# Accumulating scatters of a mixture-of-experts stage: one chain over two tables, or one chain for each table

## The reference, cut to what matters

```
h   = RMSNorm(x) * (1 + scale_f) + shift_f            # 1032 x 1024
experts, weights = top 6 of 64 by a sigmoid router    # 6 of 64 for each token
for each block of rows that go to one expert e:
    y = (silu(rows @ w1[e]) * (rows @ w3[e])) @ w2[e] # 1024 -> 256 -> 1024
    routed[token of the row] += y * weight
x   = x + gate_f * (shared_expert(h) + routed)
out = RMSNorm(x) * g_final
```

## Time and profile before

| | |
|---|---|
| median of 3 runs | 1570.03 us (1564.13 to 1572.75) |
| the profiled execution | 1567.41 us |
| its span, from the first to the last instruction | 1565.6 us |
| granted TensorE clock, mean over the span | 0.967 of full speed |
| PE busy | 1441.4 us, 92% |
| DVE busy | 832.3 us, 53% |
| POOL busy | 492.7 us, 31% |
| moved by DMA | 369.69 MB, mean 236 GB/s |

### The profile page before, as it was taken

The page is one execution under the profiler, slowest core; times in us unless marked ns, Lnnn a source line. Parts: engine busy times, 40 slices in busy tenths (PEclk is TensorE's granted clock), DMA queues, the critical chain, the costliest instruction groups (busy, mean ns, idle before and its releaser), DMA issues.

```text
span 1565.6 us, 17523 instructions
## 1 busy us (share of the span) xinstructions
PE 1441.4 (92%) x5855; PEld 642.1 (41%) x5855; DVE 832.3 (53%) x2113; ACT 217.7 (14%) x369; POOL 492.7 (31%) x426
## 2 busy tenths in 40 slices
PE   5899999999999999989899999999989999999947
PEld 2344454554445454644333344433323333333313
DVE  1047778999979899856233333333323243333227
ACT  1111321313121321322000000000000000000003
POOL 0001010111212111215345454545544544554410
PEclk9999999999999999988899999999999999999978
DMA  9987202202121001511999999999999999999976
GB/s 333 325 315 289 84 27 97 79 32 84 41 71 41 19 29 42 170 56 49 341 307 370 364 374 366 375 363 355 367 369 351 375 362 375 331 341 329 375 228 247
DMA packets 93436, 369.69 MB, mean 236 GB/s; under 512 B 17741, under 2 KB 29425, under 8 KB 68207
## 3 DMA queue, kind: packets, MB, share of 16 engines
q1 hardware_dynamic: 69383, 304.29, 50.0%
q0 software_dynamic: 23968, 64.35, 16.5%
HBM read 323.10 MB, written 62.13 MB: 246 GB/s over the span
## 4 chain that ended last, share of the span: by engine, by line
DMA 39%; PE 28%; DVE 19%; issue 8%; SPq 4%; ACT 2%; POOL 0%; POOLq 0%; DVEq 0%; ACTq 0%
DMA acc_rows<-W,kT 18%; DMA acc_rows<-xr,kT 13%; PE U L652 9%; DVE cv L1260 7%; PE R L705 7%; PE U L862 4%; DMA acc_rows<-xr,shared_f 4%; SPq L401 2%; PE R L878 2%; DMA W<-in_w_ada 1%; DMA x_t<-h_rows,q_r 1%; PE R L616 1%; SPq L408 1%; PE U L811 1%; DVE R L1272 1%
## 5 line engine op out<-in xcount | busy, mean ns | idle before, releaser
L652 PE MATMUL U<-W,hT 128*128 128x512 f32 x864 | 385.4, 600 | 1.2 <-issue 1.2
L1260 DVE SCALAR_TENSOR_TENSOR cv<-win,cw,cv 128x128 f32<-128x128 f32 x960 | 254.9, 345 | 1.4
L878 PE MATMUL R<-W,glu 128*32 128x512 f32 (+2 forms) x1024 | 240.9, 597 | 1.3 <-DVE glu L1552 1.3
L862 PE MATMUL U<-W,hT 128*128 128x512 f32 (+2 forms) x784 | 236.4, 606 | 5.1 <-issue 5.1
L652 PEld LDWEIGHTS U<-W,hT 128*128 128x128 f32 x864 | 162.5, 193 | 188.3 <-issue 188.3
L862 PE MATMUL U<-W,cat 128*32 128x512 f32 (+2 forms) x1264 | 236.2, 603 | 0.0
L1539 DVE STREAM_TRANSPOSE hT<-x_t 128x1024 f32<-128x1024 f32 x33 | 67.2, 2036 | 207.4 <-DMA x_t<-h_rows,q_r 174.1
L1539 DVE STREAM_TRANSPOSE cat<-W 128x1024 f32<-128x1024 f32 x33 | 67.7, 2051 | 198.9 <-DMA W<-h_rows,q_r 198.9
L878 PEld LDWEIGHTS R<-W,glu 128*32 128x32 f32 (+2 forms) x1024 | 83.9, 138 | 151.4 <-issue 149.9
L1734 POOL DMA_INDIRECT W<-h_rows,q_r x128 | 129.1, 1009 | 53.5 <-issue 53.5
L862 PEld LDWEIGHTS U<-W,hT 128*128 128x128 f32 (+2 forms) x784 | 90.8, 158 | 126.7 <-issue 125.4
(11 more groups left out here) (293 smaller groups left out, 1173.6 us busy)
## 6 DMA issues: line engine op xcount, KB each, us to landing
W<-in_w SPq DMA_DIRECT2D x192, 1024.0 KB, 17.2
W<-in_w_ada SPq DMA_DIRECT2D x24, 1024.0 KB, 8.8
W<-in_w_in SPq DMA_DIRECT2D x6, 2048.0 KB, 20.0
W<-acc_rows SPq DMA_DIRECT2D x16, 512.0 KB, 9.7
h_rows<-xr SPq DMA_DIRECT2D x9, 512.0 KB, 2.7
x_t<-in_x_prompt SPq DMA_DIRECT2D x8, 512.0 KB
W<-in_w_out SPq DMA_DIRECT2D x1, 4096.0 KB, 17.2
xr<-in_x_prompt SPq DMA_DIRECT2D x8, 512.0 KB
```

Source lines behind the costliest of these rows:

```text
L652: last = mm(U[BANK[g]][:, :], hT[:, k, :], w_in[:, k, 512 * g:512 * g + 512], start=k == 0, stop=k == KT - 1)
L862: last = mm(U[1][cols, :], xgT[z][:, k, cols], w13[:, :, k, :], start=k == 0, stop=k == KT - 1)
L878: last = mm(R[cols, 512 * half:512 * half + 512], hidT[:, f, cols], weights[:, at:at + 512], start=f == 0, stop=f == FT - 1)
L1260: ins = v.scalar_tensor_tensor(cv[:, c, :], win[:, c, w:w + P], cw[:, c, w:w + 1], cv[:, c, :], ALU.mult, ALU.add)
```

## The change

The two tables become two tensors, `acc_rows[0]` and `acc_rows[1]`, and a plan `PARTS` says for each block which of its quarters go to which table. A block of one expert (and one of the shared expert) goes as one piece to the table that the plan counts free first. A mixed block is cut by its owners into two pieces, the larger first, one to each table, and is scattered by two transfers: each gets all 128 rows and a list of row numbers of its own in which the other piece's rows are far out of bounds. Rows out of bounds are skipped (`oob_is_err=False`), and since the bound is now the number of tokens, filling rows are skipped too. A piece waits only for the pieces before it in the same table (`DONE` counts them), and DVE's evacuation of block x waits until all pieces of block x-2 have landed. In the last stage tiles 0 and 1 get a semaphore each; DVE adds the two halves of tile 0 itself, and PE starts with tile 1. The row numbers of both tables are made by one DVE operation of twice the columns, from a constant of twice the size. SP's waits for the end of the scatters, and the further rounds, count the pieces in the same way.

```diff
+def pieces(x):
+    u = EXEC[x][0]
+    owners = [None] * 4 if u is None else [s for s, _ in QUARTERS[4 * u:4 * u + 4]]
+    first = owners.count(owners[0])
+    return [(0, first)] + [(first, 4 - first)] * (first < 4)
+
+def chains():
+    parts, done, busy = [], [], [0, 0]
+    for x in range(NX):
+        cut = sorted(pieces(x), key=lambda piece: -piece[1])
+        nearer = 0 if busy[0] <= busy[1] else 1
+        taken = [((nearer + i) % 2, at, n) for i, (at, n) in enumerate(cut)]
+        for table, _, n in taken:
+            busy[table] = max(busy[table], 11 * x) + 3 + 2 * n
+        parts.append(taken)
+        done.append(tuple(sum(table == c for block in parts for table, _, _ in block) for c in range(2)))
+    return parts, done
+
+PARTS, DONE = chains()
...
-        acc_in = win_in[0:TP // 2]
-        rows_summed = win_in[TP // 2]
+        acc_in = [win_in[0], win_in[1]] + [win_in[2 + i // 2] for i in range(TP - 2)]
+        acc_there = [16 + 32, 16 + 32] + [16 + 64] * (TP - 2)
+        rows_summed = win_in[5]
...
-        acc_rows = scratch("acc_rows", (2 * TABLE, D))
+        acc_rows = [scratch(f"acc_rows{i}", (TABLE, D)) for i in range(2)]
...
-        slot_i = kT[:, 0, 0:64].bitcast(I32)
+        slot_i = kT[:, 0, 0:2 * NU].bitcast(I32).rearrange("p (c u) -> p c u", c=2)
...
-        slot_base = k_d[:, 192:192 + NU]
+        slot_base = k_d[:, 192:192 + 2 * NU].rearrange("p (c u) -> p c u", c=2)
...
             for i in range(TP):
-                sp.dma_start(acc_t[i], acc_rows[P * i:P * i + P, :]).then_inc(acc_in[i // 2], 16)
-                sp.dma_start(odd_t[i], acc_rows[TABLE + P * i:TABLE + P * i + P, :]).then_inc(acc_in[i // 2], 16)
+                sp.dma_start(acc_t[i], acc_rows[0][P * i:P * i + P, :]).then_inc(acc_in[i], 16)
+                sp.dma_start(odd_t[i], acc_rows[1][P * i:P * i + P, :]).then_inc(acc_in[i], 16)
...
-            for i in range(TP):
-                pe.wait_ge(acc_in[i // 2], 16 + 64)
+            for i in range(1, TP):
+                pe.wait_ge(acc_in[i], acc_there[i])
...
             def blk_y(x):
                 dve.wait_ge(y_done, x + 1)
-                dve.wait_ge(scattered[x % 2], 16 * (x // 2))
+                for c in range(2):
+                    if x > 1 and DONE[x - 2][c]:
+                        dve.wait_ge(scattered[c], 16 * DONE[x - 2][c])
...
-            v.tensor_tensor(slot_i[:, 0:NU], X[:, 0:NU], slot_base, ALU.add).then_inc(slot_ready, 1)
+            v.tensor_tensor(slot_i, X[:, 0:NU].unsqueeze(1).to_broadcast([P, 2, NU]), slot_base, ALU.add).then_inc(slot_ready, 1)
...
             for i in range(TP):
-                dve.wait_ge(sum_done, i + 1)
-                ins = v.tensor_tensor(acc_t[i], (X, R)[i % 2][:, :], gt_f, ALU.mult)
+                if i == 0:
+                    dve.wait_ge(acc_in[i], acc_there[i])
+                    link(v.tensor_tensor(acc_t[i], acc_t[i], odd_t[i], ALU.add))
+                    ins = v.tensor_tensor(acc_t[i], acc_t[i], gt_f, ALU.mult)
+                else:
+                    dve.wait_ge(sum_done, i)
+                    ins = v.tensor_tensor(acc_t[i], (X, R)[i % 2][:, :], gt_f, ALU.mult)
...
             def scatter(x):
                 u, n = EXEC[x]
-                at = shared_i[:, 4 * NT + n:4 * NT + n + 1] if u is None else slot_i[:, u:u + 1]
                 pool.wait_ge(y_evac, x + 1)
-                if x > 0:
-                    pool.wait_ge(scattered[1 - x % 2], 16 * ((x + 1) // 2))
-                pool.indirect_dma_start(acc_rows, bass.IndirectOffsetOnAxis(ap=at, axis=0), y_sbs[x % 2], None,
-                                        bounds_check=2 * TABLE - 1, oob_is_err=True,
-                                        compute_op=ALU.add).then_inc(scattered[x % 2], 16)
+                before = [0, 0] if x == 0 else list(DONE[x - 1])
+                for c, first, n in PARTS[x]:
+                    if before[c]:
+                        pool.wait_ge(scattered[c], 16 * before[c])
+                    before[c] += 1
+                    at = shared_i[:, 4 * NT + EXEC[x][1]:4 * NT + EXEC[x][1] + 1] if EXEC[x][0] is None else slot_i[:, c, EXEC[x][0]:EXEC[x][0] + 1]
+                    pool.indirect_dma_start(acc_rows[c], bass.IndirectOffsetOnAxis(ap=at, axis=0), y_sbs[x % 2], None,
+                                            bounds_check=TOKENS - 1, oob_is_err=False,
+                                            compute_op=ALU.add).then_inc(scattered[c], 16)
...
-        "slot_base": np.array([[TABLE * (QUARTERS[4 * u + p // 32][0] % 2) for u in range(NU)] for p in range(P)]),
+        "slot_base": skips(),
...
+def skips():
+    far = np.full((P, 2, NU), 8.0 * TABLE)
+    for x, (u, _) in enumerate(EXEC):
+        if u is not None:
+            for c, at, n in PARTS[x]:
+                far[32 * at:32 * at + 32 * n, c, u] = 0.0
+    return far.reshape(P, 2 * NU)
```

More of the change, by code:

```diff
@@ L172, in build @@
         ring_in = [sem(f"ring_in{r}") for r in range(RING + 1)]
-        acc_in = win_in[0:TP // 2]
-        rows_summed = win_in[TP // 2]
+        acc_in = [win_in[0], win_in[1]] + [win_in[2 + i // 2] for i in range(TP - 2)]
+        acc_there = [16 + 32, 16 + 32] + [16 + 64] * (TP - 2)
+        rows_summed = win_in[5]
+        assert TP == 8
         sum_done, gated = sem("sum_done"), sem("gated")
@@ L462, in _ @@
                 for x in range(2):
-                    sp.dma_start(acc_rows[bass.ds(i * 2 * P + TABLE * x - 4 * P, 2 * P), :], t["zeros"]).then_inc(spare_in, 16)
+                    sp.dma_start(acc_rows[x][bass.ds(i * 2 * P - 4 * P, 2 * P), :], t["zeros"]).then_inc(spare_in, 16)
                 load_next(i)
@@ L521, in _ @@
             sp.dma_start(disp, t["disp"]).then_inc(disp_in, 16)
-            sp.dma_start(slot_base, t["slot_base"]).then_inc(disp_in, 16)
+            sp.dma_start(k_d[:, 192:192 + 2 * NU], t["slot_base"]).then_inc(disp_in, 16)
             sp.wait_ge(x2_ready, NT)
@@ L556, in _ @@
                         b = rd * NE + s
-                        sp.wait_ge(scattered[1], 8 * NX)
-                        sp.wait_ge(scattered[0], 8 * NX + 16 * b)
+                        sp.wait_ge(scattered[1], 16 * DONE[-1][1])
+                        sp.wait_ge(scattered[0], 16 * DONE[-1][0] + 16 * b)
                         sp.sem_inc(sp_free, 1)
@@ L578, in _ @@
                 sp.dma_start(g_s[rows], t["g_final"].rearrange("(c n) -> c n", n=SW)).then_inc(sample_in, 16)
-            sp.wait_ge(scattered[0], 8 * NX + 16 * NE * rounds)
+            sp.wait_ge(scattered[0], 16 * DONE[-1][0] + 16 * NE * rounds)
             sp.sem_inc(sp_free, 1)
-            sp.wait_ge(scattered[1], 8 * NX)
-            sp.dma_start(acc_s, in_pieces(acc_rows[SEQ:TOKENS, :])).then_inc(sample_in, 16)
-            sp.dma_start(odd_s, in_pieces(acc_rows[TABLE + SEQ:TABLE + TOKENS, :])).then_inc(sample_in, 16)
+            sp.wait_ge(scattered[1], 16 * DONE[-1][1])
+            sp.dma_start(acc_s, in_pieces(acc_rows[0][SEQ:TOKENS, :])).then_inc(sample_in, 16)
+            sp.dma_start(odd_s, in_pieces(acc_rows[1][SEQ:TOKENS, :])).then_inc(sample_in, 16)
             for i in range(TP):
-                sp.dma_start(acc_t[i], acc_rows[P * i:P * i + P, :]).then_inc(acc_in[i // 2], 16)
-                sp.dma_start(odd_t[i], acc_rows[TABLE + P * i:TABLE + P * i + P, :]).then_inc(acc_in[i // 2], 16)
+                sp.dma_start(acc_t[i], acc_rows[0][P * i:P * i + P, :]).then_inc(acc_in[i], 16)
+                sp.dma_start(odd_t[i], acc_rows[1][P * i:P * i + P, :]).then_inc(acc_in[i], 16)
             for i in range(TP):
@@ L1786, in _ @@
                         pool.sem_inc(pool_free, 1)
-                        pool.indirect_dma_start(acc_rows, bass.IndirectOffsetOnAxis(ap=slot_cur, axis=0), y_sbs[0], None,
-                                                bounds_check=2 * TABLE - 1, oob_is_err=True,
+                        pool.indirect_dma_start(acc_rows[0], bass.IndirectOffsetOnAxis(ap=slot_cur, axis=0), y_sbs[0], None,
+                                                bounds_check=TOKENS - 1, oob_is_err=False,
                                                 compute_op=ALU.add).then_inc(scattered[0], 16)
```

## The result

The changed kernel takes 1573.83 us (median of 19 runs, 1570.24 to 1579.82) beside 1568.83 us of the kernel before on the same chips (19 runs, 1564.13 to 1574.75). The ratio is 1.0034, with a 95% interval from 1.0022 to 1.0047: no faster, a little slower. Predicted were 1550.

What follows compares the result with a forecast made beforehand. PE was taken as the bound, with 20.2 us of waits for DVE caused by chained scatters delaying gathers on POOL. −16.0 − 0.5 − 3.4 = −19.9 from 1567.4 gave 1547.5; the median lies 2.6 higher, so 1550, range 1540 to 1567.

Steps and rivals of the forecast that it cites:

- the landing of the second piece: Mixed blocks' second scatter: lands 8.5 us after its start, so the next block's gathers still move up by 2.1 us.
- the other case that I had named: Whole blocks behind mixed ones: if the second piece took 10.4 us by itself, gathers would move up by 0.2 us only.
- the 4.3 us behind mixed blocks: Expert stage: half of the 8.6 us of PE's waits shared to the 28 mixed blocks was to go.
- the forecast with nothing taken off: Case that skipped rows still cost their time: same as the forecast, since the 1224 filling rows were counted at 0.
- 11.6 counted for all 38 one-piece blocks: Expert stage: 38/66 of PE's 20.2 us of waits for DVE, 11.6 us, was to go whole.
- DMA is full: Rival, expert stage: freeing the order moves nothing, only bytes count; −12 − 3.9 us, about 1554; chance 0.17.
- The second piece makes it slower: Rival, mixed blocks: POOL still waits and each second piece delays gathers by 1.91 us; +38, about 1608; chance 0.11.
- Filling rows: Scatters: 1224 rows, 5.0 MB, no longer written; counted at 0, with 12.4 to 19.9 us if DMA is the bound.
- The last stage: After the expert stage: DVE adds tile 0 and takes tile 1 sooner; −3.4 us, bounds −2.5 and −4.5.
- The end of the stage: Last scatters of blocks 64 and 65, both mixed: between +1.3 and −2.7 us, taken as −0.5.
- The signs named: Right: 94 scatters, DVE at tile 1 about 14 us after SP's first load, PE's DVE waits under 5 us.
- The rule against the split: First rival, two-piece scatters: transfers to disjoint partition halves serialize, so the split earns no rate; only order and bytes count.

Runs made afterwards that it cites:

- own rows: Changed kernel with each piece scattered from its own partitions only, no row skipped for the other piece's sake; 1550.83 us, 0.989 of the kernel before.
- the last stage alone: The kernel before with only the last-stage edit (DVE adds tile 0, PE starts with tile 1), scatters as before; ratio 0.9983 to the kernel before.
- second only: Changed kernel with own rows in the second pieces alone, first pieces keeping their skipped rows; ratio 1.0063 to the kernel before.

## Why the prediction was wrong

**The step that failed** is the landing of the second piece: "The two pieces together carry one block's rows, so I let the second land when the whole block would have", 8.5 us after its start. They carry one block's data, but two blocks' rows, and a skipped row is still a packet. It measured 11.1 to 11.7 us, worse than the other case that I had named ("Were the piece to take 10.4 us by itself") and set aside. So nothing came of the 4.3 us behind mixed blocks, nor of the 2.1 us that gathers were to move up behind 21 whole ones; 19 of the 21 whole blocks behind a mixed one still waited for a landing, 4.95 us on POOL in the mean of the 21. (I had all 21 behind a second piece; by the plan three of them, 38, 51 and 62, follow the first piece. And the blocks with a piece that follows one from the block just before are not 27 but these 21 and all 28 mixed ones.)

**Skipped rows** I took for neutral: "the forecast with nothing taken off, since I counted 0 there". I had thought of the 1224 filling rows, which the change takes away, and not of the 3584 rows that the same mechanism adds. Without them the kernel measures 1550.83 us, 0.989: the forecast's size, but in part by luck. PE's waits for DVE do go as forecast, from 20.2 to 0.9 us, but those for weights rise from 5.1 to 17.8, for which the sum had no term; and some 8 of the 17 us gained come from filling rows that are not written, which I had counted at 0 too.

**One-expert blocks.** The gain came, 9.0 us from block 14 to 28, of 11.6 counted for all 38 one-piece blocks. But 4.2 of it went back at block 29, and with own rows 11.0 of 11.2. This is the second step that failed: the sum took each wait of PE that goes as time gained, and in no run here that frees the order under the full load is block 29 reached more than 3.9 us sooner than before. I had read the earlier trace rows as "PE waited for weights only once" and so put "DMA is full" at 0.17. The waits for DVE in the same rows hung on the same load: with half of the down weights left out, 4.0 of 17.9 us stayed. The row that said so was there, a share of 1.02 at 366 GB/s in the earlier trace rows. The Trainium skill, page "DMA: Bandwidth & Descriptors", section "Specifications", lists 368 GB/s as the vendor's cost-model derate. The windows of the changed kernel above lie on both sides of it, with 364 and 372 at shares of 1.01 and 1.03.

**"The second piece makes it slower"** had the right direction and the wrong place. POOL's wait ahead of second pieces is 0.51 us in the mean of 28, below the 0.7 that I had set as the point from which it decides. The wait stands one scatter further on, ahead of the whole block, which I had let start 9.4 us after the second piece. In the rows of POOL above it started 12.16 us after it.

**Filling rows** were counted at 0. In the changed kernel that holds within its uncertainty; with own rows, where DMA sets the pace, they are worth 8 us.

**The ends.** The last stage: −3.4 counted, −3.3 measured in the trace of the changed kernel, −2.1 in that of the last stage alone. The end of the stage: −0.5 counted, +0.9 measured; the two pieces of a block go out 1.9 us apart, and the last one, with only its twin still in the queue, takes 6.2 us with its skipped rows (1523.15 to 1529.38). With own rows in both it takes 5.2, so with no weights and no gathers beside them the skipped rows of this pair cost 1.0 us.

**The signs named** told the cases apart: scatters 94, DVE at tile 1 after 14.0 us, both right; PE's waits for DVE at 24 us and not under 5, with landings above 11 us, wrong.

**The rule against the split.** The Trainium skill, page "DMA: Bandwidth & Descriptors", section "Rules for kernel authors", says that two transfers to disjoint halves of the partitions serialize. It holds here as far as it goes: the split earned no rate, with 364 GB/s from 850 to 1150 us against 366 before. What it doesn't touch is the order. Whether two pieces of own rows beat the one scatter of a mixed block is not shown: with filling rows written in both kernels it is 0.994 against 0.9961, within their intervals.

Open are the delay of the weights in "second only", and why the landings of pieces with fewer packets are sooner by so much under load, 2.6 and 1.7 us, and by only 1.0 at the end.

## What to carry to other kernels

Count what a queue is given in rows and packets as well as in bytes: an index list with entries out of bounds saves data and no packets, so cut the list where partitions allow it. Where DMA is at a share of 1.0, as in blocks 15 to 28 here, a wait removed in one place can be paid back at the next transfer that is late; take bytes out in one run before crediting an order with a gain. And what stands behind a late transfer in an in-order queue decides whether its lateness costs anything.

## What the hardware showed that was not expected

Rows skipped by the bounds check of an indirect transfer leave one packet each under 512 B in the trace (22997 over the whole execution with 3584 rows skipped for the other piece, 19445 with 32), and the page's count of bytes written to HBM includes them as if written (76.81 MB against 62.26). Removing them in one of two neighbouring transfers gave nothing, removing them in both 1.44%.
